# Samples' attention in another order: keys and queries split first, V last, p turned in the middle part, scores waiting for each quarter of the keys

## Chip, cores and metric

The kernel runs on one core of a Trainium2 chip. The metric is the device time of one execution in microseconds (us). The engines are TensorE (PE in the rows, its weight loads PEld), VectorE (DVE), ScalarE (ACT), GpSimd (POOL) and SyncE (SP), which issues nearly all DMAs.

## What is computed

One layer of a hybrid encoder for a prompt (1,024 tokens) and for eight sampled sequences (16 tokens each, with caches of 512 keys and values). The change touches only the attention of the eight sampled sequences:

```
# forgetting attention, 8 heads x 64: 512 cached keys and values and 16 new ones
s = q . k * 64**-0.5 + c[query] - c[key];  s = -inf where key is after query
o_fox = softmax(s) @ v
# attention over memory, 4 heads x 128, 256 tokens from a cache
o_mem = softmax(qm . mk * 128**-0.5) @ mv
```

Around it stand a projection of all 1,152 tokens by `w_in`, the same two attentions of the prompt, a pooling branch, a gated merge of the three branches, and a feed-forward layer.

## The kernel before

Every product in f32 is made of three: each operand is split into a high part (a rounded copy, made by ScalarE) and a low part (the difference, made by VectorE), and TensorE multiplies high by high, high by low and low by high (`COMBOS`). So each operand of an attention passes ScalarE and then VectorE before TensorE can use it.

The work is a list written out by hand, `plan`: blocks of a 128-column product (kinds `qm`, `gate`, `br` and others), each walked in halves (12 matmuls of 384 columns in a half of `qm` and `gate`). `beside` hangs further steps on halves: at such a half each engine first runs its own part of those steps, then its part of the half. The order on an engine is the order of the code; engines meet only at semaphores (`wait_ge`, `then_inc`). TensorE therefore works through: steps, half product, steps, half product.

The attention of the samples is `sample(k, s)`: k is 0 for the forgetting attention (tiles `foxs_...`) and 1 for memory (`mems_...`), and s runs over `3 * NB + 1` steps, which gives each sequence i (called a batch below) three parts, on three halves in a row:

- Part 0. TensorE: `scores()` of i (four quarters of the keys, three products each, and for k = 0 the 16 new keys with each), then `values()` of i - 1. VectorE reads the scores with the bias (k = 0) or takes their maximum, masks the output of i - 1 (`masked_out`, tile `om`) and takes the reciprocal of the sum. ScalarE: exp, then scaling of p.
- Part 1. TensorE: `turned_out()` of i - 1 and `turn_keys(i + 1, 0)`, two quarters of the next keys. ScalarE: `out()`, `keys_hi(i + 1, 0)`, high half of V (`foxs_v_hi`, `foxs_vn_hi`). VectorE: `out()`, `keys_lo(i + 1, 0)`, low half of V, `queries(i + 1)`.
- Part 2. TensorE: `turn()` of p and `turn_keys(i + 1, 1)`, the other two quarters. ScalarE: high part of turned p, `keys_hi(i + 1, 1)`. VectorE: low part of turned p, `keys_lo(i + 1, 1)`. SyncE: `load_values(i + 1)`, which waits for V's low half (`v_lo`), and `load_keys(i + 2)`, which waits for the turned keys (`kt_over`).

`kraw`, `vraw`, `bias`, `p`, `pt` and `kt` have one buffer each. `refill` splits the prompt's attention output (`branch_raw`) in four steps, one batch each. Scores of i wait for all four quarters before the first matmul: `pe.wait_ge(sa["kt_lo"], 4 * c + 4)`.

## Time and profile before

| | us |
|---|---|
| time, median of 3 runs (lowest, highest) | 2254.65 (2243.49, 2261.84) |
| the profiled execution: its own time | 2257.44 |
| its span, first to last instruction | 2255.7 |
| TensorE busy in the span | 2122.0 (94%) |
| VectorE busy | 993.3 (44%) |
| ScalarE busy | 688.3 (31%) |
| mean granted clock of TensorE | 0.961 |

Busy times are sums over an engine's instructions. The granted clock is the share of TensorE's full clock that it was given, as a mean over a stretch. Line numbers L890 and the like are those of the kernel before.

### The profile page before, as it was taken

The page shows a single profiled execution, that of the slowest core. Times are in us where ns is not written, and L with a number is a line of the kernel's source. Part 1 is how long each engine was busy: PE and PEld are TensorE (multiplying, and loading weights), DVE is VectorE, ACT ScalarE, POOL GpSimd, SP SyncE. Part 2 cuts the span into 40 slices and gives each one's busy share as a digit, 9 for nine tenths or more (in the row PEclk, how much of TensorE's full clock was granted, in tenths as well). Part 3 has the DMA queues.
Part 4 walks back from the last instruction along what each step waited for, and adds up shares of the span by engine and source line. Part 5 has one row for each costly group of instructions (what it writes and reads, how often), then busy time and mean ns, then how long its engine had stood idle before and what let it go on. Part 6 is the DMA issues. An engine that isn't in the chain of part 4 may idle for free.

```text
span 2255.7 us, 29158 instructions
## 1 busy us (share of the span) xinstructions
PE 2122.0 (94%) x12111; PEld 2027.9 (90%) x12111; DVE 993.3 (44%) x1876; ACT 688.3 (31%) x1214; POOL 7.0 (0%) x37
## 2 busy tenths in 40 slices
PE   6898999989998888888989999999999999999997
PEld 6897888978887777888989999999999999999997
DVE  6454424343343332555543344644434444344434
ACT  7225425244353332455522233311111111111102
POOL 0000000000000000000000000000000000000000
PEclk9999999999998776999999999999999999999999
DMA  6511121121115333133442332111110111112012
GB/s 185 147 33 59 53 75 30 65 60 65 36 37 192 106 101 123 58 113 108 146 129 72 86 94 70 38 34 52 29 57 29 52 33 48 47 33 61 24 52 93
DMA packets 211784, 164.75 MB, mean 73 GB/s; under 512 B 14399, under 2 KB 190527, under 8 KB 211142
## 3 DMA queue, kind: packets, MB, share of 16 engines
q1 hardware_dynamic: 211653, 162.90, 23.6%
q8 instruction: 96, 1.57, 0.3%
q14 instruction: 35, 0.28, 0.0%
HBM read 133.36 MB, written 29.51 MB: 72 GB/s over the span
## 4 chain that ended last, share of the span: by engine, by line
PE 55%; DVE 2%; ACT 2%; issue 1%; DMA 0%; SPq 0%; DVEq 0%; ACTq 0%
PE ps L1040 51%; PE ps L903 1%; PE ps L890 1%; PE ps L917 0%; PE ps L977 0%; PE ps L1001 0%; PE ps L866 0%; DMA branch_raw<-o_mem 0%; ACT mem_p L1173 0%; ACT w_hi L408 0%; DVE prod L1817 0%; DVE fin_y L1876 0%; DVE prod L1822 0%; PE ps L1121 0%; ACT fin_sq L1439 0%
## 5 line engine op out<-in xcount | busy, mean ns | idle before, releaser
L1040 PE MATMUL ps<-act_hi,w_hi 128*128 128x384 f32 x1824 | 628.5, 345 | 0.2 <-DVE w_lo L415 0.2
L1040 PE MATMUL ps<-act_hi,w_lo 128*128 128x384 f32 x1824 | 617.8, 339 | 0.0
L1040 PE MATMUL ps<-act_lo,w_hi 128*128 128x384 f32 x1824 | 617.7, 339 | 0.0
L1040 PEld LDWEIGHTS ps<-act_hi,w_hi 128*128 128x128 f32 x1824 | 348.6, 191 | 3.4 <-issue 2.5
L1040 PEld LDWEIGHTS ps<-act_lo,w_hi 128*128 128x128 f32 x1824 | 348.7, 191 | 0.4
L1040 PEld LDWEIGHTS ps<-act_hi,w_lo 128*128 128x128 f32 x1824 | 348.2, 191 | 0.0
L408 ACT ACTIVATE w_hi<-w_raw 128x512 fp32r<-128x512 f32 (+1 forms) x181 | 152.8, 844 | 381.1 <-PE ps L1040 375.7
L1040 PE MATMUL ps<-ff_hi,w_hi 128*128 128x384 f32 x768 | 259.5, 338 | 0.0
L1040 PE MATMUL ps<-ff_lo,w_hi 128*128 128x384 f32 x768 | 259.4, 338 | 0.0
L1040 PE MATMUL ps<-ff_hi,w_lo 128*128 128x384 f32 x768 | 259.4, 338 | 0.0
L415 DVE TENSOR_TENSOR w_lo<-w_raw,w_hi 128x512 fp32r<-128x512 f32 (+1 forms) x181 | 174.6, 965 | 147.4 <-ACT w_hi L408 147.4
L1857 DVE TENSOR_TENSOR h<-ps,h 128x384 f32<-128x384 f32 x192 | 107.0, 558 | 232.9 <-PE ps L1040 232.9
L1339 ACT ACTIVATE ff_hi<-ff_r 128x384 fp32r<-128x384 f32 x96 | 50.4, 526 | 325.7 <-DVE ff_r L1846 325.7
L1040 PEld LDWEIGHTS ps<-ff_hi,w_hi 128*128 128x128 f32 x768 | 144.2, 188 | 0.0
L1040 PEld LDWEIGHTS ps<-ff_lo,w_hi 128*128 128x128 f32 x768 | 144.2, 188 | 0.0
L1040 PEld LDWEIGHTS ps<-ff_hi,w_lo 128*128 128x128 f32 x768 | 144.2, 188 | 0.0
L1846 DVE SCALAR_TENSOR_TENSOR ff_r<-ps,rstd 128x384 f32<-128x384 f32 x96 | 53.5, 557 | 185.0 <-PE ps L1040 185.0
L1040 PE MATMUL ps<-branch_hi,w_hi 128*128 128x384 f32 x288 | 101.7, 353 | 6.4 <-DVE branch_lo L1740 6.4
L1040 PE MATMUL ps<-branch_hi,w_lo 128*128 128x384 f32 x288 | 98.1, 341 | 0.0
L1040 PE MATMUL ps<-branch_lo,w_hi 128*128 128x384 f32 x288 | 98.0, 340 | 0.0
L1173 ACT ACTIVATE fox_p<-fox_p,small 128x128 f32<-128x128 f32 (+3 forms) x64 | 49.8, 778 | 145.0 <-DVE small L1582 144.9
L1582 DVE CUSTOM_DVE_ANT_0 fox_p<-ps,fox_negc 128x128 f32<-128x128 f32 (+3 forms) x64 | 48.2, 753 | 41.2 <-issue 40.7
(318 smaller groups left out, 2909.0 us busy)
## 6 DMA issues: line engine op xcount, KB each, us to landing
w_raw<-in_w_in_dram SPq DMA_DIRECT2D x45, 512.0 KB, 4.5
w_raw<-in_w_up_dram SPq DMA_DIRECT2D x32, 512.0 KB, 4.1
w_raw<-in_w_down_dram SPq DMA_DIRECT2D x64, 256.0 KB, 2.8
merged<-prod SPq DMA_DIRECT2D x48, 192.0 KB, 1.9
prev<-merged SPq DMA_DIRECT2D x48, 192.0 KB, 4.2
foxs_kraw<-in_cache_fox_k_dram SPq DMA_DIRECT2D x8, 1024.0 KB, 7.2
foxs_vraw<-in_cache_fox_v_dram SPq DMA_DIRECT2D x8, 1024.0 KB, 5.4
out_dram<-fin_y SPq DMA_DIRECT2D x9, 512.0 KB, 2.6
```

What stands on the lines that cost most here:

```text
L408: nc.scalar.activation(W[c % 2][0][:, 0:kt, :], w_raw[c % 2][:, 0:kt, :], ACT.Copy).then_inc(w_hi[c % 2], 1)
L415: nc.vector.tensor_tensor(W[c % 2][1][:, 0:kt, :], w_raw[c % 2][:, 0:kt, :], W[c % 2][0][:, 0:kt, :].bitcast(F32), ALU.subtract).then_inc( ...
L890: last = nc.tensor.matmul(ps[:, 2, 0:a.tiles * P], stat, b["kt"][y][:, j, :], start=first, stop=end)
L903: last = nc.tensor.matmul(ps[:, 4, :], b["pt"][x][:, t, :], b["v"][y][:, t, :], start=(n == 0 and t == 0), stop=end)
L1040: last = nc.tensor.matmul(bank(b)[:, 0:width], W[k][a][:, t, :], moving[z][:, t, j * width:(j + 1) * width], start=(t == 0 and n == 0), st ...
L1173: nc.scalar.activation(dst, src, ACT.Exp, bias=bias, scale=scale, accum_out=col(SUM, u)).then_inc(at_s["exp"], 1)
L1339: nc.scalar.activation(AC[s.i % 2][0][:, s.j, cols(j)], ff_r[i % 2][:], ACT.Square).then_inc(ff["hi"], 1)
L1582: nc.vector.tensor_tensor_reduce(out=fp[s % 2][:, 0:n], in0=ps[:, 0:2, :].rearrange("p a c -> p (a c)")[:, 0:n], in1=negc[:, s // QT, 0:n] ...
L1846: nc.vector.scalar_tensor_tensor(out=ff_r[i % 2][:], in0=src, scalar=0.0, in1=rstd[:, cols(j)], op0=ALU.max, op1=ALU.mult).then_inc(free, 1)
L1857: nc.vector.tensor_tensor(h, src, h, ALU.add).then_inc(free, 1)
```

## The change

In `sample` on all engines the turning and splitting of p moves from part 2 to the head of part 1; the low half of V moves from part 1 to the end of part 2 on VectorE, behind the second two quarters of the keys; the queries stay in part 1 and come right behind the first two quarters. The reciprocal comes ahead of the masked output. The turned output goes to PSUM bank 2 in place of bank 3. `scores()` waits for each quarter of the keys by itself. SyncE issues the load of the keys ahead of that of V. The `refill` steps stand on the same halves, ahead of the sample's step in place of behind it.

```diff
--- before.py
+++ after.py
@@ -166,9 +166,9 @@
     put(where[1], "first", 0, 0)
     put(where[2], "first", 0, 1)
     for s in range(3 * NB + 1):
+        if s % 3 == 0 and 2 <= s // 3 < 2 + BT:
+            put(where[3 + s], "refill", 0, s // 3 - 2)
         put(where[3 + s], "sample", 0, s)
-    for g in range(BT):
-        put(where[9 + 3 * g], "refill", 0, g)
     put(where[28], "mem_parts", 0)
     where = [(k, 1, n, x) for n in range(KT) for k, w in (("gate", 6), ("br", 3)) for x in range(w)]
     for s in range(BT * QT + 2):
@@ -558,9 +558,9 @@
                 if part == 1 and a.new and i + 1 < NB:
                     load_bias(i + 1)
                 if part == 2 and i + 1 < NB:
-                    load_values(a, i + 1)
                     if i + 2 < NB:
                         load_keys(a, i + 2)
+                    load_values(a, i + 1)
                 if a.new and s == 3 * NB - 3:
                     sp.wait_ge(sa["kt_over"], 4 * NB)
                     sp.wait_ge(kst_stored, 16 * MH)
@@ -873,17 +873,21 @@
 
                 def scores():
                     pe.wait_ge(sa["q_pad"], c + 1)
-                    pe.wait_ge(sa["kt_lo"], 4 * c + 4)
                     if i and a.new:
                         pe.wait_ge(sa["s_read"], c)
                         pe.wait_ge(sa["pt_lo"], c)
                     elif i:
                         pe.wait_ge(sa["exp"], c)
+                    if i >= 2:
+                        pe.wait_ge(sa["o_done"], c - 1)
+                    elif i:
+                        pass
                     elif a.new:
                         pe.wait_ge(at_s["pt_lo"], UNITS)
                     else:
                         pe.wait_ge(at_s["pt_lo"], UNITS + M_UNITS)
                     for j in range(4):
+                        pe.wait_ge(sa["kt_lo"], 4 * c + j + 1)
                         for n, (x, y) in enumerate(COMBOS):
                             first, end = j == 0 and n == 0, j == 3 and n == 2
                             stat = b["qpad"][x][:, j * P:(j + 1) * P]
@@ -909,12 +913,10 @@
 
                 def turned_out():
                     pe.wait_ge(sa["om"], c)
-                    if a.new and i < NB:
-                        pe.wait_ge(sa["s_read"], c + 1)
-                    elif not a.new and c >= 2:
-                        pe.wait_ge(sa["o_done"], c - 1)
+                    if i < NB:
+                        pe.wait_ge(sa["s_read" if a.new else "exp"], c + 1)
                     for j in range(4):
-                        last = nc.tensor.matmul(ps[:, 3, 256 + j * NQ:256 + (j + 1) * NQ], b["om"][:, j * P:(j + 1) * P],
+                        last = nc.tensor.matmul(ps[:, 2, j * NQ:(j + 1) * NQ], b["om"][:, j * P:(j + 1) * P],
                                                 rsel[:], start=True, stop=True)
                     last.then_inc(sa["ot_over"], 1)
 
@@ -922,11 +924,9 @@
                     pe.wait_ge(sa["p_ready"], c + 1)
                     if i:
                         pe.wait_ge(sa["om"], c)
-                    if i and a.new:
-                        pe.wait_ge(sa["o_done"], c)
                     elif a.new:
                         pe.wait_ge(at_s["o_done"], PAIRS)
-                    elif i == 0:
+                    else:
                         pe.wait_ge(at_s["o_done"], PAIRS + M_PAIRS)
                     for t in range(a.tiles):
                         last = nc.tensor.transpose(ps[:, 4, t * P:(t + 1) * P], b["p"][:, t * P:(t + 1) * P], ident[:])
@@ -942,14 +942,13 @@
                     if i == NB:
                         turned_out()
                 elif part == 1:
+                    turn()
                     if i:
                         turned_out()
                     if i + 1 < NB:
                         turn_keys(a, i + 1, 0)
-                else:
-                    turn()
-                    if i + 1 < NB:
-                        turn_keys(a, i + 1, 1)
+                elif i + 1 < NB:
+                    turn_keys(a, i + 1, 1)
 
             def mem(s):
                 def scores(u):
@@ -1237,7 +1236,7 @@
 
                 def out():
                     act.wait_ge(sa["ot_over"], c)
-                    src = ps[:, 3, 256:256 + 4 * NQ].rearrange("p (j q) -> p j q", q=NQ)
+                    src = ps[:, 2, 0:4 * NQ].rearrange("p (j q) -> p j q", q=NQ)
                     if a.new:
                         nc.scalar.activation(X[0][:, :, SEQ + (i - 1) * NQ:SEQ + i * NQ], src,
                                              ACT.Copy).then_inc(sa["o_hi"], 1)
@@ -1260,6 +1259,12 @@
                 elif part == 0:
                     out()
                 elif part == 1:
+                    act.wait_ge(sa["pt_over"], c + 1)
+                    last = nc.scalar.activation(b["pt"][0][:, 0:a.tiles, :],
+                                                ps[:, 4, 0:a.tiles * P].rearrange("p (t q) -> p t q", q=P), ACT.Copy)
+                    if a.new:
+                        last = nc.scalar.activation(b["pt"][0][0:NQ, a.tiles, :], ps[0:NQ, 3, P:2 * P], ACT.Copy)
+                    last.then_inc(sa["pt_hi"], 1)
                     if i:
                         out()
                     if i + 1 < NB:
@@ -1272,15 +1277,8 @@
                         act.wait_ge(sa["vn_in"], 16 * (c + 1))
                         last = nc.scalar.activation(b["vn"][0][:], b["vnraw"][:], ACT.Copy)
                     last.then_inc(sa["v_hi"], 1)
-                else:
-                    act.wait_ge(sa["pt_over"], c + 1)
-                    last = nc.scalar.activation(b["pt"][0][:, 0:a.tiles, :],
-                                                ps[:, 4, 0:a.tiles * P].rearrange("p (t q) -> p t q", q=P), ACT.Copy)
-                    if a.new:
-                        last = nc.scalar.activation(b["pt"][0][0:NQ, a.tiles, :], ps[0:NQ, 3, P:2 * P], ACT.Copy)
-                    last.then_inc(sa["pt_hi"], 1)
-                    if i + 1 < NB:
-                        keys_hi(a, i + 1, 1)
+                elif i + 1 < NB:
+                    keys_hi(a, i + 1, 1)
 
             def refill(k, g):
                 if g == 0:
@@ -1679,7 +1677,7 @@
                     if a.new:
                         dve.wait_ge(sa["o_hi"], c)
                         cs = slice(SEQ + (i - 1) * NQ, SEQ + i * NQ)
-                        nc.vector.tensor_tensor(X[1][:, :, cs], ps[:, 3, 256:256 + 4 * NQ].rearrange("p (j q) -> p j q", q=NQ),
+                        nc.vector.tensor_tensor(X[1][:, :, cs], ps[:, 2, 0:4 * NQ].rearrange("p (j q) -> p j q", q=NQ),
                                                 X[0][:, :, cs].bitcast(F32), ALU.subtract).then_inc(sa["o_done"], 1)
 
                 if part == 0 and i < NB and a.new:
@@ -1699,26 +1697,14 @@
                     nc.vector.tensor_reduce(col(MX, c), ps[:, 2, 0:a.tiles * P], AX_X, ALU.max).then_inc(sa["max"], 1)
                     dve.wait_ge(sa["max"], i + 1)
                     nc.vector.tensor_scalar(col(NM, c), col(MX, c), -M_SCALE, None, ALU.mult).then_inc(sa["negmax"], 1)
-                if part == 0 and i:
-                    masked_out()
                 if part == 0 and i < NB:
                     dve.wait_ge(sa["exp"], c + 1)
                     nc.vector.reciprocal(col(RC, c), col(SUM, c)).then_inc(sa["recip"], 1)
-                elif part == 0:
+                if part == 0 and i:
+                    masked_out()
+                if part == 0 and i == NB:
                     out()
                 elif part == 1:
-                    if i:
-                        out()
-                    if i + 1 < NB:
-                        keys_lo(a, i + 1, 0)
-                    dve.wait_ge(sa["v_hi"], c + 1)
-                    last = nc.vector.tensor_tensor(b["v"][1][:], b["vraw"][:], b["v"][0][:].bitcast(F32), ALU.subtract)
-                    if a.new:
-                        last = nc.vector.tensor_tensor(b["vn"][1][:], b["vnraw"][:], b["vn"][0][:].bitcast(F32), ALU.subtract)
-                    last.then_inc(sa["v_lo"], 1)
-                    if i + 1 < NB:
-                        queries(a, i + 1)
-                else:
                     dve.wait_ge(sa["pt_hi"], c + 1)
                     last = nc.vector.tensor_tensor(b["pt"][1][:, 0:a.tiles, :],
                                                    ps[:, 4, 0:a.tiles * P].rearrange("p (t q) -> p t q", q=P),
@@ -1727,8 +1713,19 @@
                         last = nc.vector.tensor_tensor(b["pt"][1][0:NQ, a.tiles, :], ps[0:NQ, 3, P:2 * P],
                                                        b["pt"][0][0:NQ, a.tiles, :].bitcast(F32), ALU.subtract)
                     last.then_inc(sa["pt_lo"], 1)
+                    if i:
+                        out()
+                    if i + 1 < NB:
+                        keys_lo(a, i + 1, 0)
+                        queries(a, i + 1)
+                elif part == 2:
                     if i + 1 < NB:
                         keys_lo(a, i + 1, 1)
+                    dve.wait_ge(sa["v_hi"], c + 1)
+                    last = nc.vector.tensor_tensor(b["v"][1][:], b["vraw"][:], b["v"][0][:].bitcast(F32), ALU.subtract)
+                    if a.new:
+                        last = nc.vector.tensor_tensor(b["vn"][1][:], b["vnraw"][:], b["vn"][0][:].bitcast(F32), ALU.subtract)
+                    last.then_inc(sa["v_lo"], 1)
 
             def refill(k, g):
                 n = k * BT + g + 1
```

TensorE between the scores of batch 1 and those of batch 2 (`rsel,foxs_om` is the turn of the output, `foxs_p` of p, `foxs_kraw` of the keys). Before:

```order
L906 MATMUL ps<-foxs_vn_hi,foxs_pt_lo 128x512
...
L917 MATMUL ps<-rsel,foxs_om 128x16 x4
L866 MATMUL ps<-ident,foxs_kraw 128x128 x8
...
L932 MATMUL ps<-ident,foxs_p 128x128 x4
L934 MATMUL ps<-ident,foxs_p 16x128
L866 MATMUL ps<-ident,foxs_kraw 128x128 x8
```

And now:

```order
L910 MATMUL ps<-foxs_vn_hi,foxs_pt_lo 128x512
...
L932 MATMUL ps<-ident,foxs_p 128x128 x4
L934 MATMUL ps<-ident,foxs_p 16x128
L919 MATMUL ps<-rsel,foxs_om 128x16 x4
L866 MATMUL ps<-ident,foxs_kraw 128x128 x8
...
L866 MATMUL ps<-ident,foxs_kraw 128x128 x8
```

The turn of p has moved ahead of the output's, one half product earlier.

VectorE in batch 2, from the turned output to the next batch's bias (`foxs_qpad` are the queries, `branch_lo<-branch_raw` is a refill step). Before:

```order
L1682 TENSOR_TENSOR branch_lo<-ps,branch_hi 128x4x16
L1636 TENSOR_TENSOR foxs_kt_lo<-ps,foxs_kt_hi 128x512 x2
L1715 TENSOR_TENSOR foxs_v_lo<-foxs_vraw,foxs_v_hi 128x2048
L1717 TENSOR_TENSOR foxs_vn_lo<-foxs_vnraw,foxs_vn_hi 16x512
L1648 CAST foxs_qpad_hi<-qs_hi 64x4x16 x2
L1648 CAST foxs_qpad_lo<-qs_lo 64x4x16 x2
L1723 TENSOR_TENSOR foxs_pt_lo<-ps,foxs_pt_hi 128x512
L1727 TENSOR_TENSOR foxs_pt_lo<-ps,foxs_pt_hi 16x128
L1636 TENSOR_TENSOR foxs_kt_lo<-ps,foxs_kt_hi 128x512 x2
L1688 TENSOR_TENSOR foxs_bias<-foxs_bias,mask_new 128x16
```

And now:

```order
L1709 TENSOR_TENSOR foxs_pt_lo<-ps,foxs_pt_hi 128x512
L1713 TENSOR_TENSOR foxs_pt_lo<-ps,foxs_pt_hi 16x128
L1680 TENSOR_TENSOR branch_lo<-ps,branch_hi 128x4x16
L1634 TENSOR_TENSOR foxs_kt_lo<-ps,foxs_kt_hi 128x512 x2
L1646 CAST foxs_qpad_hi<-qs_hi 64x4x16 x2
L1646 CAST foxs_qpad_lo<-qs_lo 64x4x16 x2
L1634 TENSOR_TENSOR foxs_kt_lo<-ps,foxs_kt_hi 128x512 x2
L1725 TENSOR_TENSOR foxs_v_lo<-foxs_vraw,foxs_v_hi 128x2048
L1727 TENSOR_TENSOR foxs_vn_lo<-foxs_vnraw,foxs_vn_hi 16x512
L1733 TENSOR_TENSOR branch_lo<-branch_raw,branch_hi 128x1024
```

V's low half stood between the two pairs of key quarters and now stands behind the second pair; p's low half stood just ahead of that pair and now leads.

ScalarE in the same batch (`tok` is the store copy of a half product). Before:

```order
L1242 ACTIVATE branch_hi<-ps 128x4x16
L1230 ACTIVATE foxs_kt_hi<-ps 128x512 x2
L1270 ACTIVATE foxs_v_hi<-foxs_vraw 128x2048
L1273 ACTIVATE foxs_vn_hi<-foxs_vnraw 16x512
L1277 ACTIVATE foxs_pt_hi<-ps 128x512
L1280 ACTIVATE foxs_pt_hi<-ps 16x128
L1230 ACTIVATE foxs_kt_hi<-ps 128x512 x2
```

And now:

```order
L1263 ACTIVATE foxs_pt_hi<-ps 128x512
L1266 ACTIVATE foxs_pt_hi<-ps 16x128
L1241 ACTIVATE branch_hi<-ps 128x4x16
L1229 ACTIVATE foxs_kt_hi<-ps 128x512 x2
L1275 ACTIVATE foxs_v_hi<-foxs_vraw 128x2048
L1278 ACTIVATE foxs_vn_hi<-foxs_vnraw 16x512
L1229 ACTIVATE foxs_kt_hi<-ps 128x512 x2
```

V's high half stays between the two pairs; only p's copies have moved, to the head.

## Rows read from the trace of the kernel before

**Rows 1.** TensorE's waits from 690 to 915: waited for, us in total, times, longest
```profile
PE ps L890 <- DVE foxs_kt_lo L1636: 23.4, 7, 3.8
PE ps L903 <- DVE foxs_pt_lo L1727: 2.0, 1, 2.0
```

**Rows 2.** Cut at first scores, batches 0, 1, 2, 7: us, busy of five engines, clock, DMA
```profile
693.50:710.25 16.75, 12.94 (x82) 12.06 (x82) 8.08 (x18) 7.41 (x13) 0.00 (x0) 0.96 0.38 136
710.25:736.03 25.78, 22.52 (x105) 18.81 (x105) 9.87 (x20) 8.20 (x14) 0.00 (x0) 0.83 0.40 125
736.03:766.94 30.91, 27.63 (x105) 22.27 (x105) 9.97 (x20) 8.70 (x15) 0.00 (x0) 0.67 0.25 88
...
879.37:907.29 27.92, 25.93 (x88) 20.55 (x89) 6.58 (x12) 5.36 (x9) 0.00 (x0) 0.63 0.42 140
```

**Rows 3.** Timeline of TensorE, batch 0: start, us, engine, line, operation [idle before]
```profile
697.61 0.42 PE L1040 MATMUL ps<-act_hi,w_hi 128*128 128x384 f32 x1
...
699.78 1.04 PE L866 MATMUL ps<-ident,foxs_kraw 128*128 128x128 f32 x8
```

**Rows 4.** The same, batch 1 at the full clock, up to batch 2's first score
```profile
719.94 1.21 PE L903 MATMUL ps<-foxs_v_lo,foxs_pt_hi 128*128 128x512 f32 x4
...
721.51 1.19 PE L903 MATMUL ps<-foxs_v_hi,foxs_pt_lo 128*128 128x512 f32 x4
...
723.05 0.45 PE L1040 MATMUL ps<-act_hi,w_hi 128*128 128x384 f32 x1
...
729.10 0.60 PE L932 MATMUL ps<-ident,foxs_p 128*128 128x128 f32 x4
...
729.64 1.04 PE L866 MATMUL ps<-ident,foxs_kraw 128*128 128x128 f32 x8
...
736.03 0.75 PE L890 MATMUL ps<-foxs_kt_hi,foxs_qpad_hi 128*128 128x512 f32 x1 [3.26 <-DVE foxs_kt_lo L1636]
```

**Rows 5.** Timeline of ScalarE, batch 2, middle and last part
```profile
758.69 1.91 ACT L1270 ACTIVATE foxs_v_hi<-foxs_vraw 128x2048 fp32r<-128x2048 f32 x1
...
761.01 0.57 ACT L1277 ACTIVATE foxs_pt_hi<-ps 128x512 fp32r<-128x512 f32 x1
...
761.65 1.05 ACT L1230 ACTIVATE foxs_kt_hi<-ps 128x512 fp32r<-128x512 f32 x2
```

**Rows 6.** Timeline of VectorE, the same batch
```profile
761.14 2.29 DVE L1715 TENSOR_TENSOR foxs_v_lo<-foxs_vraw,foxs_v_hi 128x2048 fp32r<-128x2048 f32 x1 [1.50 <-ACT foxs_vn_hi L1273]
763.35 0.67 DVE L1717 TENSOR_TENSOR foxs_vn_lo<-foxs_vnraw,foxs_vn_hi 16x512 fp32r<-16x512 f32 x1
...
765.57 1.27 DVE L1636 TENSOR_TENSOR foxs_kt_lo<-ps,foxs_kt_hi 128x512 fp32r<-128x512 f32 x2
```

**Rows 7.** Timeline of all engines, batch 0: read of the scores and scaling of p
```profile
697.93 0.71 DVE L1694 CUSTOM_DVE_ANT_0 foxs_p<-ps,foxs_bias 128x528 f32<-128x528 f32 x1
...
699.74 0.74 ACT L1259 ACTIVATE foxs_p<-foxs_p,small 128x528 f32<-128x528 f32 x1 [0.23 <-DVE small L1706]
```

**Rows 8.** Tile foxs_vraw: V's load, issues and us from issue to landing
```profile
L533 SPq DMA_DIRECT2D foxs_vraw<-in_cache_fox_v_dram x8: 383/383/511, 678.4 to 876.5; - x8
...
DMA to landing us min/median/max: 5.2/5.4/8.9
```

**Rows 9.** Timeline of all engines, batch 0 of the memory attention
```profile
1052.04 0.60 PE L866 MATMUL ps<-ident,mems_kraw 128*128 128x128 f32 x4
...
1052.59 0.51 ACT L1259 ACTIVATE mems_p<-mems_p,small 128x256 f32<-128x256 f32 x1 [0.23 <-DVE small L1706]
...
1056.76 0.44 PE L866 MATMUL ps<-ident,mems_kraw 128*128 128x128 f32 x2 [1.79 <-DVE mems_kt_lo L1636]
```

**Rows 10.** Timeline of TensorE at the kernel's start, eight transposes each
```profile
18.70 1.94 PE L770 MATMUL ps<-ident,xs 128*128 128x128 f32 x8 [1.95 <-DVE act_lo L1468]
...
23.75 1.07 PE L770 MATMUL ps<-ident,xs 128*128 128x128 f32 x8 [0.77 <-DVE act_lo L1468]
```

**Rows 11.** Two microseconds after the stage's end: columns as in rows 2
```profile
914.00:916.00 2.00, 2.00 (x7) 2.00 (x8) 0.23 (x1) 0.74 (x2) 0.00 (x0) 0.50 0.90 284
```

## The prediction

> **What bounds the kernel now.** I read the share of each engine first (the table of times: TensorE busy 94% of the span), then TensorE's waits in the stage that the change touches, then that stage cut at each batch's first score matmul, then the timelines of single batches on TensorE, ScalarE and VectorE.
>
> From 693.50 (first score matmul of batch 0) to about 911.9 (end of the last values) the kernel runs the eight sampled sequences of the forgetting attention, called batches here, between half products of the big projection. TensorE waits there almost only in front of the scores: 7 waits, 23.4 us in all, each for VectorE's last `kt_lo`; one more of 2.0 us stands in front of the last values [rows 1]. The waits are the smaller part. Cut at each first score, a batch takes 26 to 31 us, and the granted clock averages 0.63 to 0.83 in it, though it is 0.96 in batch 0, which has no wait ahead of it [rows 2]. The timeline shows the order: TensorE idles 3.26 us ahead of 736.03 [rows 4], the scores behind it start at or within about 1 us of the lower level (1.2 GHz of the two, 1.2 and 2.4), and the full clock returns only during the values or the products behind them. That is so behind all seven waits. Behind no shorter wait of this stage but one (rival B) did it fall.
>
> So what is to be read is the length of a batch without the wait and at the full clock. Scores: batch 0 starts them at 693.50 and its next product at 697.61, 4.11 us [rows 2, 3]. Values: at the full clock 1.55 for five matmuls, three times, 4.65 (719.94 to 723.05 has two of them) [rows 4]. The rest (three half products, the turns of p, of the output and of the keys) runs from 723.05 to 736.03 less 3.26 of wait, 9.72 [rows 4]. Sum 18.48 us.
>
> **The change part by part.** No instruction is added or dropped; waits and places differ. I count from the first score of a batch at the full clock.
>
> *TensorE.* Scores to 4.1, values to 8.8, half product to 11.0, then p is turned (0.54, 729.10 to 729.64 [rows 4]) to 11.5, the output to 12.3, two quarters of the keys to 13.1, half product to 15.3, the other two quarters to 16.1, half product to 18.5.
>
> *When is p ready?* Its chain is VectorE's read of the scores, exp, reciprocal, scaling: in batch 0 from the scores' end at 697.61 to 700.48 (699.74 plus 0.74), 2.9 us [rows 3, 7]. In the changed order the reciprocal stands ahead of the masked output, so this chain no longer waits for the values. TensorE asks for p 6.9 us after the scores (values and half product): spare 4 us. Batch 0 has no values: it asks at 699.78 [rows 3] and waits until 700.5, cost 0.75.
>
> *ScalarE.* The copies of turned p (0.64, 761.01 to 761.65 [rows 5]) now come first: 11.6 to 12.3, output to 12.5, first two key copies to 13.7, V and new V (758.69 to 761.01, 2.3 [rows 5]) to 16.0, with the store copy of a half product (0.5) in every second batch 16.5, third key quarter by 17.1, fourth by 17.6.
>
> *VectorE.* Now the low half of V (2.29 and 0.67 overlapped, about 2.9 [rows 6]), the queries and p's low half all precede the last two key quarters: from 761.14 to 765.57 plus 1.27, and this is what TensorE waits for [rows 6]. After the change the V part stands behind them, and the third and fourth quarters end about 0.65 behind their copies, at 17.7 and 18.2. TensorE wants the third at 18.5 plus two quarters of the scores (half of 4.11), 20.5: spare 2.8, even with the wait for all four put first spare 0.3. So the order removes the wait, and the waits by quarter give the margin.
>
> *What is late next.* V's low half ends at 21.1; the values want it at 22.6: spare 1.5. In four batches the refill's VectorE step on 1,024 columns (half of V's 2,048, so about 1.2) follows, to 22.3, still before the scores' end at 22.6. In the last batch no keys follow: its last values would come at 15.3 plus 1.6, 16.9, and V's low half is ready at about 18.3; a wait of 1.4 in place of the 2.0.
>
> *SyncE's queue.* K's load is put ahead of V's. K is freed at 16.1 and wanted at 30.8. V's load waits for its low half at 21.1; behind it in the queue stand the store of a memory-query tile and, each second batch, a weight load that is wanted 12 half products later. V lands 5.4 us later, at worst 8.9 [rows 8], at 26.5 to 30.0, and ScalarE wants it at 18.5 plus 13.7, 32.2: spare 2.2 at worst.
>
> *Three more waits per batch inside the scores*, sixteen batches: between 0 and 0.1 us each when they are already met. A half product of 12 matmuls with its own waits takes 2.17 [rows 3], 0.1 over twelve steady starts. That is 0 to 4.8; I take 1.5, since nothing is late there.
>
> *The memory attention's eight batches* (1048 to 1141) run at the full clock and hardly wait. In its batch 0 TensorE would ask for p at 1052.04 and it is ready at 1053.1: a cost of 1.1; the wait of 1.79 in front of the keys there goes, since the copies and low halves of the first two quarters come earlier [rows 9]. I take 0, bounds minus 2 and plus 4.
>
> **The sum.** Now: 911.9 less 693.5 is 218.4. After: batch 0 is 16.75 less 3.81 of wait [rows 2], plus 0.75, 13.7; batches 1 to 6, 6 times 18.48, 110.9; batch 7 16.9 and 1.4; last values 4.65. Together 147.6. Gain 70.8, less 1.5: 69.3. The profiled execution took 2257.44, which gives 2188; the median is 2.8 under that execution, so I forecast **2187 us**.
>
> **Rivals.**
> *A, the forecast*: the clock stays up once the waits are gone. For it: batch 0, and the memory attention with the same mix of work and no long wait.
>
> *B, the waits go but the clock still falls once per batch.* The new order puts 2.1 us of turns in a row (p, output, keys), between products. Against: in batch 1 the output's and the keys' turns stood together and the clock held. For: at 914 to 916 the clock was at the lower level (0.50) after only 2.0 and 0.8 us of idle time with the values and the output's turn around them [rows 11], so short turns and light work can do it too. Only the idle time itself is then saved: 23.4 less 0.75, and the last values' 0.6; 2257 less 23 is **2234**.
> The start of the kernel bears on it: with nothing but transposes and waits under 2 us before, eight transposes took 1.94 us at 18.70 and 1.07 at 23.75 [rows 10], so the clock rose on transposes alone. The Trainium skill, TensorE: Matmul & The Clock Gate, Part 4: PE-mode transpose, says that transposes do not count as busy time for the clock; by that rule B would be likelier than A, but this trace does not agree at its start, and I follow the trace.
>
> *C, slower: the clock stays at the lower level through whole batches.* A batch at the lower level has no dense stretch long enough, and without a wait nothing changes on it. A batch's work times its clock is about constant: 30.91 less 3.26 at 0.67 is 18.5 [rows 2]. The present mean of batches 1 to 7 is 28.1 (710.25 to 907.29), so C decides when a gapless batch's mean clock is below 18.5 through 28.1, 0.66; at 0.50 throughout it is 37 us a batch, 7 times 8.9, 62 more: up to **2318**. Against: after every one of the seven falls the clock came back within the same batch.
>
> *D, V's load becomes the bound.* It costs from a landing 11 us after issue and makes the kernel slower only from about 20; the longest here is 8.9 [rows 8]. A few late ones give 2195 to 2210.
>
> *E, residual waits on a queue that I misread*, under 2 us each so that the clock holds: 8 times 1 to 2, 2195 to 2205.
>
> **How the numbers follow.** A 0.76, its range 2176 to 2198 (the bounds of the added waits, of the memory attention, and some 4 us for how runs of this kernel differ). D and E 0.12, B 0.08, C 0.03, no change 0.01. The range 2173 to 2210 takes A, most of D and E. What a measurement can tell from no change is about 1%, 22.5 us, so A, D and E count as faster, 0.88; B (0.9% under) mostly as the same; C as slower. With some spread of B to both sides: 0.90, 0.06, 0.04.
>
> **What would show it.** Waits of the scores for `kt_lo` gone or below 1 us in total; the granted clock at 1.00 from 700 to the end of the stage; the starts of the scores 18 to 19 us apart; the last values ending near 843 in place of 912; K's DMA issued before V's; a wait of about 0.7 for p in batch 0 and 1.4 before the last values. Starts 25 us apart with a clock near 0.8 mean B, over 28 mean C, and ScalarE waiting for V's DMA means D. The forecast fails most plainly if the clock falls without any wait ahead of it, which I take from few rows.

## The result and the profile after

The changed kernel takes **2186.56 us** (median of 4 runs, 2185.37 to 2186.86). The kernel before, run beside it, took 2255.39 (4 runs, 2243.49 to 2261.84). The ratio is 0.969, 95% interval 0.965 to 0.973: 3.1% faster. The forecast was 2187. The profiled execution took 2186.78 against 2257.44 before, so 70.7 us went where 69.3 were forecast. One execution of e4 below (10,156 us) and one of the kernel before beside e1 to e4 (4,056 us) were slow beyond anything else and are left out of the ranges and ratios.

TensorE's waits of the changed kernel between 690 and 850, to be read beside [rows 1] (engine and line that waited, for what, us in total, times, longest):

```profile
PE ps L985 <- ACT mem_p L1184: 2.1, 1, 2.1
PE ps L907 <- DVE foxs_vn_lo L1727: 1.4, 1, 1.4
PE ps L919 <- DVE foxs_om L1674: 0.8, 1, 0.8
PE ps L932 <- ACT foxs_p L1258: 0.6, 1, 0.6
```

No row for the scores is left: 7 waits and 23.4 us are gone. (`mem_p` belongs to the next attention.) Cut at the first scores of batches 0, 1, 2 and 7 and at the last values, with a last row for what follows (columns as in [rows 2]: window, us, busy us of TensorE, its weight loads, VectorE, ScalarE, GpSimd, granted clock, DMA share, GB/s):

```profile
691.93:705.43 13.50, 12.94 (x82) 12.06 (x82) 4.89 (x15) 6.92 (x12) 0.00 (x0) 1.00 0.37 121
705.43:723.57 18.14, 18.14 (x105) 15.49 (x105) 9.37 (x21) 9.10 (x16) 0.00 (x0) 1.00 0.54 176
723.57:741.71 18.14, 18.14 (x105) 15.48 (x105) 10.43 (x22) 8.02 (x14) 0.00 (x0) 1.00 0.49 151
...
814.30:832.35 18.05, 16.61 (x90) 13.69 (x89) 9.38 (x15) 5.86 (x10) 0.00 (x0) 1.00 0.69 239
832.35:839.31 6.96, 6.96 (x15) 3.71 (x15) 0.00 (x0) 0.00 (x0) 0.00 (x0) 0.61 0.00 0
839.31:842.00 2.69, 1.91 (x10) 1.83 (x9) 0.69 (x1) 0.00 (x0) 0.00 (x0) 0.50 0.32 97
```

In batches 1 to 6 the window's length and TensorE's busy time are the same number: the engine doesn't idle, and it runs at the full clock (2.4 GHz) in all of them. Before, batch 2 took 30.91 us at a clock of 0.67 with 3.3 us idle; now 18.14. The stage lasts 147.4 us (691.93 to 839.31), and lasted 218.4: 71.0 less, which is all of the gain. (The memory attention gives 2.4 more, and the rest of the kernel is 2.7 longer.) Within the stage the clock falls once, in the last values (0.61, then 0.50).

How close it is shows on VectorE in batch 2 (start, us, line, operation, idle before and who ended it), beside [rows 6]:

```profile
735.97 0.69 DVE L1709 TENSOR_TENSOR foxs_pt_lo<-ps,foxs_pt_hi 128x512 fp32r<-128x512 f32 x1 [2.97 <-ACT foxs_pt_hi L1266]
...
737.10 1.29 DVE L1634 TENSOR_TENSOR foxs_kt_lo<-ps,foxs_kt_hi 128x512 fp32r<-128x512 f32 x2
...
740.37 1.29 DVE L1634 TENSOR_TENSOR foxs_kt_lo<-ps,foxs_kt_hi 128x512 fp32r<-128x512 f32 x2 [1.27 <-ACT foxs_kt_hi L1229]
741.58 2.28 DVE L1725 TENSOR_TENSOR foxs_v_lo<-foxs_vraw,foxs_v_hi 128x2048 fp32r<-128x2048 f32 x1
743.77 0.67 DVE L1727 TENSOR_TENSOR foxs_vn_lo<-foxs_vnraw,foxs_vn_hi 16x512 fp32r<-16x512 f32 x1
```

The fourth quarter ends at 741.66, and batch 3's first score starts at 741.71. V's low half now lies behind that start, under the scores, and ends at 744.44, 1.3 us before the values that need it (745.72). In a batch with a store copy it is 0.7 (763.19 to 763.88), so this spare is the next to run out. On ScalarE the copy of V runs without a wait ahead of it, so V's load doesn't bound anything:

```profile
736.47 1.09 ACT L1229 ACTIVATE foxs_kt_hi<-ps 128x512 fp32r<-128x512 f32 x2 [0.32 <-PE ps L866]
737.45 1.92 ACT L1275 ACTIVATE foxs_v_hi<-foxs_vraw 128x2048 fp32r<-128x2048 f32 x1
...
739.77 1.05 ACT L1229 ACTIVATE foxs_kt_hi<-ps 128x512 fp32r<-128x512 f32 x2
```

### The profile page after: what moved, and what is told of

Same layout as the page of the kernel before. It is cut to its first block, busy times and chain, and to the rows that moved or that the text cites. A ratio compares the mean times of both kernels' runs of the same rounds, so it can differ in the third digit from the quotient of the medians.

```text
span 2185.0 us, 29163 instructions
## 1 busy us (share of the span) xinstructions
PE 2078.0 (95%) x12111; PEld 1997.4 (91%) x12111; DVE 993.8 (45%) x1876; ACT 690.1 (32%) x1214; POOL 6.9 (0%) x37
## 4 chain that ended last, share of the span: by engine, by line
PE 65%; ACT 3%; DVE 3%; issue 2%; DMA 1%; SPq 0%; DVEq 0%; ACTq 0%
PE ps L1039 56%; PE ps L894 2%; PE ps L907 2%; PE ps L866 1%; PE ps L919 1%; DMA merged<-prod 0%; PE ps L910 0%; PE ps L816 0%; PE ps L976 0%; ACT w_hi L408 0%; PE ps L832 0%; PE ps L1120 0%; PE ps L1000 0%; DVE prod L1814 0%; DMA branch_raw<-o_mem 0%
```

## Experiments

Each time is a median of 4 to 10 executions, and each ratio is to the kernel before, run beside it. The questions: which part of the change carries the gain, whether it is the waits themselves or the clock, and what is left.

### Which part carries it

**e1_four_first**: the changed kernel with one wait for all four quarters.

```
+                    pe.wait_ge(sa["kt_lo"], 4 * c + 4)
                     for j in range(4):
-                        pe.wait_ge(sa["kt_lo"], 4 * c + j + 1)
```

> The changed kernel with one wait for all four quarters of the keys ahead of the scores, as before, and everything else changed. My theory (the order of the work takes the wait away, the waits by quarter only give margin): in the trace of the changed kernel the fourth quarter's low half ends at 741.66 in batch 2 and the scores start at 741.71, in a batch with a store copy it ends at 760.41 and they start at 759.86; so waits of 0 and 0.5 us in turn, the clock holds, 2187 to 2190 us. The rival (the waits by quarter carry the gain): waits of 2 us or more, the clock falls, 2230 us or more.

Measured: 2190.71 us (2187.81 to 2192.50), ratio 0.9705 (0.9659 to 0.9751). TensorE's waits for the last quarter in the trace:

```profile
PE ps L894 <- DVE foxs_kt_lo L1634: 1.6, 3, 0.5
```

Three batches wait half a microsecond each. The spare of 0.3 us that I had worked out for a single wait is 0.05 us in the changed kernel's batch 2 (741.66 to 741.71). In the other kind of batch ScalarE makes the store copy (0.46 at 757.91) ahead of the last key copies, the fourth quarter ends at 760.41, and the first score starts at 759.86: minus 0.55. The waits by quarter cover just that. Of the 4.1 us between the medians the traces show 2.8 in the stage (111.7 us from batch 1's first score to batch 7's, for 108.9 in the changed kernel). The whole spans differ by 1.1 only (2186.1 and 2185.0), since the clock then held through e1's last values, which take 4.62 us in place of 6.96.

**e2_quarters_only**: the old order, with the waits by quarter (the edit of e1 turned round).

> The kernel before with waits by quarter in the scores as its only edit. Before, TensorE was ready at 763.68 and the third and fourth quarter's low halves ended at 766.2 and 766.84. Two quarters of the scores fill 2.05 us of that, so about 0.55 us of wait is left in front of the third quarter. If the length of the idle stretch is what matters, the clock holds and nearly the whole gain comes from this edit alone: about 0.6 more a batch than the changed kernel, 2188 to 2196 us. If the order of the work is what is needed, 2235 us or more.

Measured: 2251.64 us (2231.13 to 2256.16), ratio 0.996 (0.992 to 1.000). I was wrong by some 60 us. The ten executions fall into two groups: six took 2251.5 to 2256.2 at a mean granted clock of 0.954 to 0.958, four took 2231.1 to 2236.4 at 0.965 to 0.969. So one program costs 20 us more or less by the clock that it is granted. The trace is of the longer kind. Waits, and VectorE ahead of batch 2's scores:

```profile
PE ps L890 <- DVE foxs_pt_lo L1727: 15.1, 7, 2.8
```

```profile
731.05 2.29 DVE L1715 TENSOR_TENSOR foxs_v_lo<-foxs_vraw,foxs_v_hi 128x2048 fp32r<-128x2048 f32 x1 [1.50 <-ACT foxs_vn_hi L1273]
733.26 0.67 DVE L1717 TENSOR_TENSOR foxs_vn_lo<-foxs_vnraw,foxs_vn_hi 16x512 fp32r<-16x512 f32 x1
733.86 0.38 DVE L1648 CAST foxs_qpad_hi<-qs_hi 64x64 fp32r<-64x64 f32 x2
...
734.68 0.69 DVE L1723 TENSOR_TENSOR foxs_pt_lo<-ps,foxs_pt_hi 128x512 fp32r<-128x512 f32 x1
735.29 0.27 DVE L1727 TENSOR_TENSOR foxs_pt_lo<-ps,foxs_pt_hi 16x128 fp32r<-16x128 f32 x1
735.49 1.27 DVE L1636 TENSOR_TENSOR foxs_kt_lo<-ps,foxs_kt_hi 128x512 fp32r<-128x512 f32 x2
```

The scores want two more things than keys: the padded queries, and the low half of turned p, since the new rows' scores go to the bank that turned p is read from. Both stand behind V's low half. TensorE was free at 733.59 and started at 735.81, 0.25 behind the last piece of `pt_lo`. So 8 of the 23 us of idle time go, but 2.2 us and more in one piece is left in six of the seven batches, and the clock falls within 2 us behind each of these. Behind the seventh, of 1.18 us, it didn't. The row of before named `kt_lo` because it came last; the next one, 1.3 us earlier, was hidden behind it.

**e3_v_last_only**: the old order, with one step moved on VectorE: V's low half behind the second pair of keys.

```
-                    dve.wait_ge(sa["v_hi"], c + 1)
-                    ... V's low half, new V's low half
                 ...
                     if i + 1 < NB:
                         keys_lo(a, i + 1, 1)
+                    dve.wait_ge(sa["v_hi"], c + 1)
+                    ... V's low half, new V's low half
```

> The kernel before with V's low half moved behind the second two key quarters on VectorE as its only edit (p stays late, one wait for all four quarters). The quarters end 2.9 us earlier, so a wait of 0.3 to 0.5 us is left of 3.26: the clock holds, 2188 to 2196 us. The rival (p's turn must move too): a wait of over 1.5 us, and 2220 us or more.

Measured: 2196.94 us (2195.23 to 2198.63), ratio 0.9734 (0.9688 to 0.9780). TensorE's waits, and two batches cut at their first scores:

```profile
PE ps L890 <- issue: 4.2, 7, 0.9
PE ps L866 <- DVE foxs_kt_lo L1636: 3.1, 1, 3.1
PE ps L903 <- DVE foxs_vn_lo L1730: 2.5, 1, 2.5
```

```profile
727.02:745.67 18.65, 18.38 (x104) 15.47 (x105) 9.78 (x21) 8.32 (x15) 0.00 (x0) 1.00 0.43 140
745.67:764.93 19.26, 18.40 (x105) 15.48 (x105) 10.84 (x22) 9.29 (x16) 0.00 (x0) 1.00 0.52 174
```

("issue" means that the trace names nobody who released it; the row of 3.1 stands ahead of the stage.) This one move gives 58 of the 69 us. 0.3 to 0.9 us of idle time is left ahead of each batch, in turn, and the clock stays at 1.00 through it. The longer of the two was more than I expected (0.3 to 0.5).

**e4_p_early_only**: the changed kernel without that move: V's low half in the middle part ahead of the queries, V's load ahead of K's, one wait; p is still turned and copied early.

> The changed kernel with V's low half back between the two pairs of key quarters, V's load ahead of K's, and one wait for all four quarters: what is left of the change is p's turn in the middle part. VectorE then ends the fourth quarter about 3.0 us after TensorE asks: the idle stretch stays, the clock falls behind it, 2240 to 2257 us. The rival (p's turn is the part that helps): 2190 to 2200 us.

Measured: 2268.47 us (2259.87 to 2270.41), ratio 1.0056 (1.0031 to 1.0081). The scores wait as before:

```profile
PE ps L894 <- DVE foxs_kt_lo L1634: 21.6, 7, 3.2
```

The early turn of p alone gives nothing, and the kernel is half a per cent slower, with 1.8 us less of idle time than before. Its first and third batch, cut at first scores, behind waits of 3.18 and 3.07 us:

```profile
711.83:733.27 21.44, 18.37 (x104) 15.43 (x105) 10.03 (x20) 9.27 (x15) 0.00 (x0) 1.00 0.48 150
...
757.92:788.66 30.74, 27.67 (x104) 22.21 (x105) 11.10 (x22) 9.27 (x15) 0.00 (x0) 0.67 0.33 107
```

Behind the longest wait of all seven the clock held. Behind the last five, of 3.07 each, it was low for some 20 us each time; in the kernel before that is so behind three of seven. The profiled execution was the fastest (mean granted clock 0.959). The others, at 0.953 to 0.957, took 7 to 11 us more.

**e10_v_last_quarters**: e3 with the waits by quarter, to close what e2 had left open.

> The old order with two edits at once: V's low half behind the second key pair on VectorE, and the scores waiting quarter by quarter. V last alone measured 2196.9 with waits of 0.2 to 0.9 us in front of the scores (4.2 us in all, 7 times) at a clock of 1.00; waits by quarter on the old order measured 2251.6, because p's low half and the queries stood behind V's as well. My reading: with V out of the way the fourth quarter is the only late one, so the waits by quarter remove it: waits in front of and inside the scores under 1 us in all, 2197 less 4, 2193, range 2190 to 2196. Rival: p's low half, which stands only one step ahead of the last key pair, is then what is late, waits stay at 0.3 to 0.6 us each, and the time stays at 2195 to 2198.

Measured: 2191.79 us (2190.15 to 2198.86), ratio 0.9734 (0.9707 to 0.9760). The cut at first scores:

```profile
764.43:782.74 18.31, 18.31 (x105) 15.65 (x105) 10.37 (x22) 8.08 (x14) 0.00 (x0) 1.00 0.41 143
782.74:801.19 18.45, 18.31 (x105) 15.44 (x105) 10.25 (x21) 9.51 (x16) 0.00 (x0) 1.00 0.49 166
```

With V out of the way the waits by quarter remove what e3 had left: 18.3 to 18.5 us a batch in place of 18.65 and 19.3, and no wait for the scores is listed. Alone they give 4 us of 2255 (e2). On top of V last they give 5 by the medians, though the ranges overlap and the two ratios, each to the kernel before of its own rounds, are the same. The traces say 3.3: 111.4 us from batch 1's first score to batch 7's in place of 114.7. All the rest of the change (the early turn of p, the order of the two loads, the reciprocal) is worth the remaining 5 at most. Part of it is the load order, which no run tests by itself: with V's load still ahead of K's, e10 waits 1.2 us for K's load in the stage, and the changed kernel never does.

### Is it the waits or the clock?

The forecast rests on the claim that 23 us of idle time cost 69. These three put idle time back into the changed order, in front of each batch's first score, by letting the scores also wait for a step of V's low half that VectorE does anyway.

```
                     if i and a.new:
+                        pe.wait_ge(sa["v_lo"], c)
+                    if i and a.new:
                         pe.wait_ge(sa["s_read"], c)
```

That is **e5_wait_v_low**. **e6_wait_v_part** waits for the same step without the new rows' part (a semaphore `v_mid`, counted up by the step of 2,048 columns). **e11_wait_v_half** splits that step into two of 1,024 columns and waits for the first:

```
-                    last = nc.vector.tensor_tensor(b["v"][1][:], b["vraw"][:], ...)
+                    half = a.tiles // 2
+                    last = nc.vector.tensor_tensor(b["v"][1][:, 0:half], b["vraw"][:, 0:half], ...)
+                    if a.new:
+                        last.then_inc(v_mid, 1)
+                    last = nc.vector.tensor_tensor(b["v"][1][:, half:], b["vraw"][:, half:], ...)
```

> The changed kernel with one wait added: the scores of the forgetting attention wait for the whole low half of V, which ends 2.7 us (in a batch with a store copy 3.25 us) after TensorE would start them. So an idle stretch of the old length stands in the new order, seven times. If the clock falls with the length of the stretch: a batch as long as before, 2235 to 2257 us, clock 0.6 to 0.85 in each. If it was something else in the old order: idle time alone, 7 times 3.0, 2208 us at clock 1.00.

> The same with a shorter stretch: the scores wait for V's low half without the 16 new rows, 2.1 us (with a store copy 2.65 us). Waits of up to 2.0 us stood before without a fall of the clock in this stage except one. If it holds here: 2186.6 and 7 times 2.4, 2203 us. If it falls behind some of them: each costs about 7 us more, up to 2250 us. Open which; I lean to some of them falling.

> The changed kernel, with V's low half split into two steps of 1,024 columns on VectorE (one more instruction per batch of the sampled attention and of the memory attention) and the scores of the sampled attention waiting for the first of them. The wait for all of V without the new rows left 2.1 and 2.7 us of idle time in turn and a mean clock of 0.86 in a batch, 2226; this one should leave 0.9 to 1.7 us in front of each batch's scores, some 9 us in all. If the clock falls only behind longer idle times, the batches keep 1.00, last 19.1 to 19.7 us and the time is 2186.6 plus 9 plus up to 1 for the extra steps, 2195 to 2198. Rival: 1.5 us of idle is enough (one wait of 1.45 us in front of the last values was followed by a fall, though a turn and a second wait stood behind it), then each batch loses some 3.5 us more and the time is 2215 to 2225. If only the longer of the two falls, 2205 to 2212.

| kernel | us (range) | ratio (95%) | idle ahead of the scores, in turn | clock in a batch |
|---|---|---|---|---|
| changed | 2186.56 (2185.37 to 2186.86) | 0.9691 (0.9653 to 0.9728) | 0 | 1.00 |
| e11 | 2204.02 (2196.72 to 2207.17) | 0.9772 (0.9738 to 0.9807) | 1.0 and 1.6 | 1.00; 0.85 in two |
| e6 | 2226.25 (2223.41 to 2251.71) | 0.9899 (0.9867 to 0.9931) | 2.1 and 2.7 | 0.80 to 0.86 |
| e5 | 2254.34 (2244.18 to 2261.70) | 0.9996 (0.9969 to 1.0023) | 2.7 and 3.3 | 0.66 to 0.82 |

e5 is the cleanest. It has the new order and nearly the old idle time, 20.6 us in all for 23.4, and the old time to 0.1%. So with the idle time put back the new order gains nothing that stands out of e5's own range of 17 us, and 20.6 us of idle time cost 67.8. That price isn't fixed: e4's 21.6 us left it 82 above the changed kernel, and e6 and e11 range widely by the clock granted (e6: eight executions under 2229 at 0.969 to 0.974, two at 2242 and 2252 at 0.964 and 0.958). Three batches of e5, cut at first scores:

```profile
741.91:772.25 30.34, 27.67 (x105) 22.23 (x105) 9.87 (x21) 8.91 (x15) 0.00 (x0) 0.66 0.25 87
772.25:801.58 29.33, 26.06 (x104) 20.78 (x105) 11.00 (x22) 9.27 (x15) 0.00 (x0) 0.69 0.37 114
801.58:826.86 25.28, 22.62 (x105) 18.85 (x105) 9.87 (x21) 8.91 (x15) 0.00 (x0) 0.82 0.31 104
```

The same 105 matmuls keep TensorE busy 18.14 us at the full clock and 22.6 to 27.7 here. In e6 a batch is busy 21.6, but for the first: the clock is low for some 7 us behind the wait and costs 3.5. And e11, three batches in a row (the wait ahead of them was 1.62, 1.01 and 1.62):

```profile
730.30:752.87 22.57, 21.56 (x104) 17.77 (x105) 9.94 (x22) 8.21 (x15) 0.00 (x0) 0.85 0.35 121
752.87:772.87 20.00, 18.38 (x104) 15.45 (x105) 11.07 (x23) 9.97 (x16) 0.00 (x0) 1.00 0.50 160
772.87:792.26 19.39, 18.39 (x105) 15.45 (x105) 9.94 (x22) 8.21 (x15) 0.00 (x0) 1.00 0.39 142
```

The same wait of 1.62 us, with the same work around it, was followed by a fall at 730 and at 812 and by none at 773. None of the four waits of 1.0 to 1.1 was. So my third case for e11 came nearest (only behind the longer waits, 2205 to 2212), and not behind each of those. A wait of 1.6 us costs 1.6 or about 5.

### What is left

**e7_last_v_early**: the changed kernel; in batch 7 both halves of V are split early, right behind p's scaling on ScalarE and ahead of turned p's low half on VectorE, since no keys follow.

> The changed kernel with the last batch's V split early (ScalarE in part 0, VectorE first in part 1), where no keys follow. It should take away the wait of 1.45 us ahead of the last values at 832.35 and the fall of the clock behind it (0.61, then 0.50 until about 847): 1.45 plus about half of 13 us, 2179 to 2181 us. The rival (the fall comes from the values and the output's turn, not from the wait): 2185 us.

Measured: 2182.01 us (2179.88 to 2184.21), ratio 0.9687 (0.9659 to 0.9716), 4.5 below the changed kernel, whose range it doesn't touch. The wait of 1.4 for `vn_lo` is gone, and the last values take 4.6 us (831.39 to 835.99) at a clock of 1.00, where the changed kernel takes 6.96 at 0.61. Windows of e7:

```profile
835.00:838.00 3.00, 2.22 (x14) 1.53 (x13) 0.69 (x1) 0.13 (x1) 0.00 (x0) 1.00 0.08 17
838.00:841.00 3.00, 3.00 (x12) 3.00 (x11) 0.23 (x1) 1.65 (x3) 0.00 (x0) 0.54 0.71 223
```

It still falls a little later, behind the 0.8 us ahead of the output's turn (836.77), so the rival was right in part. And the fall that the edit avoids doesn't come in every execution. Five other traces have the same wait of 1.4 to 1.5 us ahead of the same last values with the clock at 1.00 through them (e1, e4, e5, e6, e8); only the changed kernel and e11 show a fall inside them. In e1:

```profile
839.68:844.30 4.62, 4.62 (x15) 2.54 (x15) 0.00 (x0) 0.00 (x0) 0.00 (x0) 1.00 0.01 3
```

The wait itself is worth 1.45; the rest of the 4.5 is clock that another execution may not lose.

**e8_prompt_wait_later**: the changed kernel; elsewhere, in the prompt's attention, the wait for V's low half stands ahead of the first values in place of the first scores of each block.

```
-                if s == 0:
-                    emptied(pe, at["vturn", p, 0].b + 2)
                 if s < 16:
                     scores(s)
+                if s == 3:
+                    emptied(pe, at["vturn", p, 0].b + 2)
```

> The changed kernel with the same lesson used elsewhere: the prompt's forgetting attention waits for the low half of V (3.6 us, three times, and the clock falls behind each) ahead of its first scores, which need only queries and keys; here it waits ahead of its first values, three steps later. If the wait goes: 10.9 us and the low clock behind it, 2162 to 2170 us. The rival (the next product waits for the same banks of VectorE, so the wait only moves): 2180 us or more.

Measured: 2169.15 us (2165.76 to 2177.19), ratio 0.9635 (0.9601 to 0.9669), 17.4 less than the changed kernel. The profiled execution is the slowest of the four (clock 0.979, the others 0.988 to 0.991). What goes is this row of the changed kernel:

```profile
PE ps L816 <- DVE fox_v_lo L1790: 10.9, 3, 3.7
```

Of it 0.9 us comes back in front of the half products (2 waits of 0.4), so the rival, that the wait only moves, holds for that much.

**e9_both**: e7 and e8 together.

> The changed kernel with both additions: the last sampled batch's V is split early, and the prompt's attention waits for the low half of V only ahead of its first values. The two places lie some 30 us and more apart and share no buffer, so I expect their gains to add: changed kernel 2186.6, less 4.5 for the first (it measured 2182.0 alone), less 17.4 for the second (2169.2 alone), 2164.6, range 2160 to 2170. The last values of the sampled attention should show no wait and the first scores of a prompt block none for V's low half. Rival: the clock falls a little later instead (in front of the output's turn, where 0.8 us of idle stands), so one of the gains is taken back: 2169 or more.

Measured: 2167.77 us (2167.05 to 2169.28), ratio 0.9623 (0.9596 to 0.9650). It is the fastest kernel of this study, 18.8 us below the changed one. The two medians' gains added would have given 2164.6, so it is 3 us slower than that. The traces give a smaller sum: one turn of p that waits about 1.1 us in each block of the prompt comes 132.4, 134.3 and 132.2 us apart in the changed kernel (229.50, 361.94, 496.24, 628.45) and 128.4, 129.3 and 127.8 here (231.53, 359.88, 489.13, 616.89). That is 4.1, 5.0 and 4.5, 13.6 in all, of which 10 are idle time. With 13.6 for e8 and 4.5 for e7 the sum is 2168.5. So it may be that e8's median of 4 runs, with a range of 11 us, flattered it; that is argued, not shown.

## Why the prediction was right

It was right in the mechanism (case A) and in most of its terms, and the time came out too. That it came within 0.5 us is luck. The sum's own last step doesn't give 2187: 2257.44 less 69.3 is 2188.1, and 2.8 less is 2185.3. And some of its terms missed by more than that, in both directions:

- *The length of a batch*, 18.48: measured 18.14. Scores and values take 8.62 (705.43 to 714.05) for 8.76, the rest 9.52 for 9.72. Why the rows of before were a little longer was not looked into.
- *The stage*, 147.6: measured 147.4, and that closeness is luck too. The batches came out 2.4 us shorter (13.5 + 108.9 + 18.05 for 13.7 + 110.9 + 18.3), and the last values 2.3 longer (6.96 for 4.65), because the clock fell behind their wait. The prediction had that wait right (1.4; measured 1.45) but priced it as idle time alone, in the very text that says what a wait does to the clock. In e1 the last values did take 4.62 behind the same wait, so the forecast left out a risk and not a certain cost.
- *p in batch 0*: wait 0.75 forecast, 0.56 measured.
- *Spare of the fourth quarter with a single wait*: 0.3 forecast; 0.05 and minus 0.55 measured (e1). I had the fourth quarter ready 18.2 us into a batch with the store copy; it was 18.70 (741.71 to 760.41), and the waits by quarter hid that.
- *The waits inside the scores*: 1.5 allowed, none to be seen; in the changed kernel scores and values together are shorter than the sum from the old rows.
- *V's low half*: spare 1.5 forecast; 1.3, and 0.7 with a store copy, measured.
- *V's load*: landing 5.2 to 8.0 us after issue (5.2 to 8.9 before [rows 8]), and ScalarE never waited for it. Case D didn't come.
- *The memory attention*: 0, bounds minus 2 and plus 4. From its first score to its last output turn it took 94.1 us before (1048.3 to 1142.4) and 91.7 now (978.8 to 1070.5), minus 2.4, just past the bound. The wait for p is there (0.95, forecast 1.1). Of the 1.79 in front of the keys, which was to go, 0.95 is left. What the forecast didn't have is that three waits of 0.8 to 0.9 us ahead of the scores go.
- *The rest of the kernel*: nothing forecast, and 2.7 longer (3.1 more between the stage and the memory attention, 1.2 more behind it, 1.6 less ahead of the stage). Part of the 3.1 is the fall in the last values, which goes on until about 847.
- *Case B* (the clock falls even without waits) is ruled out by the clock of 1.00 in batches 1 to 6, each with 2.2 us of turns in a row (716.24 to 718.42 in batch 1). Between products such a stretch doesn't bring the clock down here. The Trainium skill, TensorE: Matmul & The Clock Gate, Part 4: PE-mode transpose, says that transposes don't count as busy time for the clock. This stretch doesn't test that, since products stand on both sides of it. The start of the kernel does, and speaks against it again, as [rows 10] did: in the changed kernel eight transposes run in 1.07 us, at the full clock, with only sixteen others and a wait before them.

```profile
10.36 3.65 PE L770 MATMUL ps<-ident,xs 128*128 128x128 f32 x16 [10.36 <-DVE xs L1459]
14.77 1.07 PE L770 MATMUL ps<-ident,xs 128*128 128x128 f32 x8 [0.76 <-DVE act_lo L1466]
```

- *Case C* didn't come either. Even e5, with the clock low for 20 us in a batch, got it back in each. Its threshold was read too high: the 0.67 in "30.91 less 3.26 at 0.67" is the mean with the wait in it, and from 736.03 to 763.66 the clock averaged 0.63, which gives 17.4 and not 18.5 (18.14 measured).

The experiments shift one reading. The prediction's text says "waits for each quarter give the margin", and e10 and e1 agree: 4 to 5 us by the medians, and 2.8 (e1) and 3.3 (e10) by the traces of the stage. But I then took them, in e2, for enough by themselves. They are not, since what a wait is put down to is only the last of several.

## What to carry to other kernels

A wait of some microseconds on TensorE is to be priced at its length plus the clock behind it: here 23 us of waits were worth 69, and the clock column of a window, not the waits' total, says so. That price varies from one execution to the next, so compare medians of several, with the granted clock beside each. Move the longest step that nobody wants yet (here 2.9 us of V's split on VectorE) behind the one that TensorE waits for, and look for every condition of the waiting instruction, since each stands behind the same step; then waits by piece give the last few microseconds. And look at a short wait at the end of a stage: up to the end of the last values, 1.45 us cost just that in five traces and 3.8 in the changed kernel's.

## What the runs showed of the hardware

- How the clock answers isn't a function of the wait's length alone. Behind 0.3 to 1.1 us it never fell ahead of a batch's scores (e3, e11, 11 waits). Behind 1.62 it fell in two of three (e11), behind 2.1 to 2.7 each time (e6), and behind 3.18 in e4 it didn't (clock 1.00 from 711.83 to 733.27). The wait of 1.45 ahead of the last values was followed by a fall within 2 us in the changed kernel, and with the same work in e8 the clock was still at 1.00 until the output's turn, 5.5 us later.
- How long it stays low differs far more than the waits do. Ahead of the scores of e6 and e11 it was some 7 us (10 behind e6's first wait). In e5, with only 0.6 us more of idle time than e6, it was 10 to 20, at the longest through scores, values and into the products:

```profile
757.86:758.86 1.00, 1.00 (x5) 0.87 (x6) 1.00 (x2) 0.00 (x0) 0.00 (x0) 1.00 0.25 94
758.86:759.86 1.00, 1.00 (x7) 0.89 (x6) 0.71 (x2) 0.00 (x0) 0.00 (x0) 0.83 0.19 39
759.86:764.86 5.00, 5.00 (x16) 4.23 (x17) 0.47 (x2) 0.00 (x0) 0.00 (x0) 0.50 1.00 322
...
765.86:766.86 1.00, 1.00 (x3) 0.52 (x3) 0.16 (x1) 0.77 (x3) 0.00 (x0) 0.76 0.61 131
```

Those are cuts of e6 behind a wait of 2.08, and the next of e5 behind one of 3.27:

```profile
741.91:742.91 1.00, 1.00 (x5) 0.86 (x5) 1.00 (x2) 0.00 (x0) 0.00 (x0) 0.74 0.08 31
742.91:761.91 19.00, 19.00 (x51) 14.09 (x51) 1.74 (x7) 1.90 (x4) 0.00 (x0) 0.50 0.16 58
761.91:762.91 1.00, 1.00 (x8) 0.92 (x6) 0.00 (x0) 0.43 (x2) 0.00 (x0) 0.52 0.00 0
```

In e6 the clock is still at 1.00 for a microsecond behind the wait, and comes back 7 us after its fall. In e5 it falls in the first microsecond and comes back 20 us later. TensorE is busy throughout in both. Two of e5's waits are different again. Ahead of 801.58 the fall comes while TensorE still idles, and the full clock is back 9 us behind the restart:

```profile
800.42:801.58 1.16, 0.00 (x0) 0.03 (x1) 1.16 (x3) 0.00 (x0) 0.00 (x0) 0.50 0.98 371
...
802.58:810.66 8.08, 8.08 (x25) 6.74 (x25) 0.87 (x5) 0.34 (x1) 0.00 (x0) 0.50 0.37 133
810.66:811.66 1.00, 1.00 (x4) 0.43 (x3) 0.16 (x1) 0.77 (x3) 0.00 (x0) 1.00 0.00 0
```

- The length goes with the moment of the fall. Over the 29 falls behind a wait for the scores in the traces of before, e4, e5, e6 and e11, the 6 that came during the wait lasted 10 us, the 14 within 0.9 us behind the restart 17 to 20, and the 9 from 1.1 to 1.7 us behind it 7, with the same work behind each. Of e2's six falls two don't fit (one just inside the wait lasted 20, one 1.9 behind the restart 17). Why the moment differs from wait to wait, and why the length goes with it, stays open: no run varied the work behind the wait with the wait held.
